# Decode step of a hybrid decoder: later loads and a split first block in the front stage, and an earlier third key load

## The reference

```
h = rms_norm(x) ; z = h @ w_in -> q_a(512), ckv(256), krope(64), u(512), qm(512), gate(2048)
q = rms_norm(q_a) @ w_q_b ; rope on q and krope ; ckv = rms_norm(ckv)
o_lat = softmax(q_lat.ckv + q_rope.krope) @ ckv     (8 heads; sample rows over a paged cache of 2048 keys)
pool  = (trailing means of u over 2, 4, 8, 16 rows - u) @ w_pool * pool_scale
mem   = rms_norm(mem_prompt) @ w_mem_kv -> k, v ; cross attention of qm (4 heads, 256 tokens)
x     = x + concat(o_lat @ w_v_b, pool, cross) * silu(gate) @ w_out ; y = rms_norm(x)
```

## Time and profile before

| what | value |
|---|---|
| median of three runs | 941.89 us |
| the profiled execution | 942.5 us, of which the span of the profile is 940.5 us and 2.0 us lie around it |
| TensorE matmuls | 917.1 us busy, 98% of the span |
| DVE, ACT, POOL | 531.7, 432.4, 43.8 us busy |
| DMA | 155.94 MB, mean 166 GB/s; some 400 GB/s in the first 38 us |

### The profile page before, as it was taken

The page is one execution under the profiler, slowest core; times in us unless marked ns, Lnnn a source line. Parts: engine busy times, 40 slices in busy tenths (PEclk is TensorE's granted clock), DMA queues, the critical chain, the costliest instruction groups (busy, mean ns, idle before and its releaser), DMA issues. The chain is left out here.

```text
span 940.5 us, 15369 instructions
## 1 busy us (share of the span) xinstructions
PE 917.1 (98%) x5649; PEld 826.2 (88%) x5649; DVE 531.7 (57%) x944; ACT 432.4 (46%) x735; POOL 43.8 (5%) x42
## 2 busy tenths in 40 slices
PE   6999999999999999999999999999999999999995
PEld 6999999999989899999999998888877888888884
DVE  6457444532475687887887558766576513134344
ACT  6764331122214566766677425677664413133301
POOL 0020003322000000000000000000100000000000
PEclk9999999999999999999999999999999999999998
DMA  9964452133452777777878626241350663224023
GB/s 363 327 241 157 134 192 92 68 111 115 174 214 98 225 241 227 237 235 229 253 236 250 224 98 220 79 146 34 117 214 28 213 213 100 80 89 157 1 90 112
DMA packets 75385, 155.94 MB, mean 166 GB/s; under 512 B 9176, under 2 KB 43545, under 8 KB 73320
## 3 DMA queue, kind: packets, MB, share of 16 engines
q1 hardware_dynamic: 74080, 147.98, 47.1%
q10 hardware_dynamic: 1232, 6.99, 2.0%
HBM read 143.56 MB, written 11.50 MB: 165 GB/s over the span
## 5 line engine op out<-in xcount | busy, mean ns | idle before, releaser
L67 PE MATMUL z<-x_hi,w_hi 128*128 128x288 f32 x512 | 153.6, 300 | 0.0
L68 PE MATMUL z<-x_lo,w_hi 128*128 128x288 f32 x512 | 150.8, 294 | 0.0
L69 PE MATMUL z<-x_hi,w_lo 128*128 128x288 f32 x512 | 150.8, 294 | 0.0
L184 ACT ACTIVATE w_hi<-w_raw 128x1024 fp32r<-128x1024 f32 (+2 forms) x62 | 64.9, 1046 | 157.8 <-PE z L69 69.3
L191 DVE TENSOR_TENSOR w_lo<-w_raw,w_hi 128x1024 fp32r<-128x1024 f32 (+2 forms) x62 | 76.8, 1239 | 76.4 <-ACT w_hi L184 76.0
L67 PEld LDWEIGHTS z<-x_hi,w_hi 128*128 128x128 f32 x512 | 96.0, 188 | 3.5 <-issue 1.1
L68 PEld LDWEIGHTS z<-x_lo,w_hi 128*128 128x128 f32 x512 | 96.1, 188 | 1.3 <-issue 0.2
L69 PEld LDWEIGHTS z<-x_hi,w_lo 128*128 128x128 f32 x512 | 96.0, 188 | 0.0
L1885 DVE TENSOR_TENSOR o_lo<-o_raw,o_hi 128x1024 fp32r<-128x1024 f32 x28 | 33.9, 1224 | 72.9 <-ACT o_hi L1735 72.8
L69 PE MATMUL z_acc<-x_hi,w_lo 128*128 128x288 f32 x256 | 75.1, 293 | 0.0
L1735 ACT ACTIVATE o_hi<-o_raw 128x1024 fp32r<-128x1024 f32 x28 | 29.5, 1059 | 72.5 <-PE pa_s L2367 26.7
(11 more groups left out here) (508 smaller groups left out, 2350.6 us busy)
## 6 DMA issues: line engine op xcount, KB each, us to landing
w_raw<-in_w_feat SPq DMA_DIRECT2D x56, 512.0 KB, 4.2
k_raw<-in_cache SPq DMA_DIRECT2D x128, 192.0 KB, 2.9
v_raw<-in_cache SPq DMA_DIRECT2D x128, 128.0 KB, 2.5
o_raw<-in_w_out SPq DMA_DIRECT2D x32, 512.0 KB, 4.1
w_raw<-in_w_mem_kv SPq DMA_DIRECT2D x16, 512.0 KB, 3.5
gate_spill<-gate_tmp SPq DMA_DIRECT2D x16, 288.0 KB, 3.2
mix<-gate_spill SPq DMA_DIRECT2D x4, 1152.0 KB, 10.4
x_nat<-in_x ACTq DMA_DIRECT2D x4, 1024.0 KB, 8.7
```

The source lines that it names most:

```text
L67: pe.matmul(out, a[0], b[0], start=start, stop=False)
L68: pe.matmul(out, a[0], b[1], start=False, stop=False)
L69: return pe.matmul(out, a[1], b[0], start=False, stop=stop)
L184: act.activation(hi_slot(s, u)[:, lo:w], s.wraw[:, u % RAW, lo:w], ACT.Copy).then_inc(s.w_hi, 1)
```

## The change

Five edits. (1) The first block of x is converted in two pieces, columns 0 to 255 and 256 to 575, on ACT and DVE, and TensorE waits for each apart. (2) Twelve products of ones (128 columns, float32, result never read) stand ahead of the first real product. (3) The natural rows are loaded from block 12 on, not from block 6, and their squares come later: row 0 at block 15, rows 1 and 2 in round 0, 3 and 4 in round 1, 5 and 6 in round 2. The mean moves to the end of round 1, root, reciprocal root, diagonal and `kv_z` to round 2, between its two memory blocks, and so does TensorE's spreading product. (4) The small tables, the pooling weights and the state are issued behind unit 8 on the sync queue, not ahead of unit 6. (5) In the middle stage quad 2 of the keys is loaded behind eight parts of `refill`, not twelve.

```diff
+FIRST_X, WARM = 2 * P, 12
 @@ sync, front
-                load_units(sp, a, s, 5, 6)
+                load_units(sp, a, s, 5, feat_unit(0) + 1)
                 for dst, src in ((psc[:], a["pool_scale_c"]),
...
-                for i in range(MIXED):
+                for i in range(1, MIXED):
 @@ scalar, front
-                        act.activation(xhi[:, k, :], xraw[:, k, :], ACT.Identity, scale=gx[:, k:k + 1]).then_inc(x_hi, 1)
-                        if k in (6, 7):
-                            load_row(k - 6)
+                        if k == 0:
+                            act.activation(xhi[:, 0, 0:FIRST_X], xraw[:, 0, 0:FIRST_X], ACT.Identity, scale=gx[:, 0:1]).then_inc(x0_hi, 1)
+                            act.activation(xhi[:, 0, FIRST_X:T], xraw[:, 0, FIRST_X:T], ACT.Identity, scale=gx[:, 0:1]).then_inc(x_hi, 1)
+                        else:
+                            act.activation(xhi[:, k, :], xraw[:, k, :], ACT.Identity, scale=gx[:, k:k + 1]).then_inc(x_hi, 1)
+                        if k in (12, 13):
+                            load_row(k - 12)
...
-                        if k in (11, 13, 15):
-                            square_row((k - 11) // 2)
+                        if k == 15:
+                            square_row(0)
...
-                    if i == 1:
+                    if i == 2:
                         act.wait_ge(chain, 1)
                         act.activation(rx[:, 2, :], rx[:, 1, :], ACT.Sqrt).then_inc(root, 1)
...
-                    if i == 0:
-                        square_row(3)
                     if i < 3:
-                        square_row(4 + i)
+                        square_row(2 * i + 1)
+                        square_row(2 * i + 2)
 @@ vector, front
                     memory(2 * i)
+                    if i == 2:
+                        dve.wait_ge(root, 2)
+                        rsqrt(dve, link, rx[:, 1, :], rx[:, 2, :], rx[:, 7, :], rx[:, 3, :])
...
                     memory(2 * i + 1)
...
-                    if i == 0:
+                    if i == 1:
                         dve.wait_ge(sq, TT)
                         link(dve.tensor_scalar(rx[:, 1, :], rx[:, 0, :], 1.0 / D, EPS, ALU.mult, ALU.add))
-                    if i == 1:
-                        dve.wait_ge(root, 2)
-                        rsqrt(dve, link, rx[:, 1, :], rx[:, 2, :], rx[:, 7, :], rx[:, 3, :])
 @@ tensor, front
+                pe.wait_ge(ident, 2)
+                for _ in range(WARM):
+                    pe.matmul(z[:, 0, 0, 0:P], s.ones[:], s.ones[:], start=True, stop=True)
                 for u in range(KV_UNITS):
                     latents(u)
                 for i in range(MIXED):
+                    memory(2 * i)
                     if i == 2:
                         pe.wait_ge(diag, TT)
...
-                    memory(2 * i)
 @@ sync, middle
-                refill(0, QPARTS)
+                refill(0, 8)
                 sp.wait_ge(normed, 8)
                 sp.wait_ge(roped, 4)
                 load_keys(2)
+                refill(8, QPARTS)
```

More of the change, by code:

```diff
@@ L255, in front_stage @@
         tail, tail_sb, st_in = sem("p_tail"), sem("p_tail_sb"), sem("p_state_in")
+        x0_hi, x0_lo = sem("p_x0hi"), sem("p_x0lo")
         w0_in, w0_hi, w0_lo, xs_hi, xs_lo, kv_low = sem("p_w0in"), sem("p_w0hi"), sem("p_w0lo"), sem("p_xshi"), sem("p_xslo"), sem("p_kvlow")
@@ L512, in _ @@
                         split_lo(dve, s, k // KV_K, k // KV_K + 1)
-                    dve.wait_ge(x_hi, k + 1)
-                    dve.scalar_tensor_tensor(out=xlo[:, k, :], in0=xraw[:, k, :], scalar=gx[:, k:k + 1],
-                                             in1=f32(xhi[:, k, :]), op0=ALU.mult, op1=ALU.subtract).then_inc(x_lo, 1)
+                    parts = ((slice(0, FIRST_X), x0_hi, x0_lo), (slice(FIRST_X, T), x_hi, x_lo)) if k == 0 else ((slice(0, T), x_hi, x_lo),)
+                    for cols, hi_done, lo_done in parts:
+                        dve.wait_ge(hi_done, k + 1)
+                        dve.scalar_tensor_tensor(out=xlo[:, k, cols], in0=xraw[:, k, cols], scalar=gx[:, k:k + 1],
+                                                 in1=f32(xhi[:, k, cols]), op0=ALU.mult, op1=ALU.subtract).then_inc(lo_done, 1)
                     if k % KV_K == KV_K - 1 or k == KD - 1:
@@ L541, in _ @@
                     memory(2 * i)
+                    if i == 2:
+                        dve.wait_ge(root, 2)
+                        rsqrt(dve, link, rx[:, 1, :], rx[:, 2, :], rx[:, 7, :], rx[:, 3, :])
+                        dve.wait_ge(ident, 3)
+                        for r in range(TT):
+                            dve.tensor_scalar(wide[:, P * r:P * r + P], s.ident[:], rx[:, 3, r:r + 1], None, ALU.mult).then_inc(diag, 1)
+                        dve.wait_ge(kv_raw, TT)
+                        for r in range(TT):
+                            m = rows(r)
+                            dve.tensor_scalar(s.kvn[0:m, r, :], s.kvn[0:m, r, :], rx[0:m, 3, r:r + 1], None, ALU.mult).then_inc(kv_z, 1)
                     memory(2 * i + 1)
@@ L640, in latents @@
                             wait_split(pe, s, u)
-                        pe.wait_ge(x_lo, k + 1)
+                        if k:
+                            pe.wait_ge(x_lo, k + 1)
+                        else:
+                            pe.wait_ge(x0_lo, 1)
                         for i in range(4):
+                            if k == 0 and P * i == FIRST_X:
+                                pe.wait_ge(x_lo, 1)
                             product(pe, kv_bank(i), (xhi[:, k, P * i:P * i + P], xlo[:, k, P * i:P * i + P]), w[kk], k == 0, k == KD - 1)
```

## The result

The changed kernel takes 947.33 us (median of six runs, 946.73 to 948.27), the kernel before, on the same chip, 941.97 us (six runs): ratio 1.0056, 95% interval 1.0047 to 1.0066. It is slower by 5.4 us, where 941.5 us was forecast: the sign and the place are those of the rival "unit 11 lands late", and the loss is larger. The profiled execution took 946.73 us (span 944.8), the lowest of its runs; that of before, 942.5 us (940.5), is above its median, so the two traces differ less, by 4.4 us (944.83 against 940.47 us).

What follows compares the result with a forecast made beforehand. TensorE, busy 98% of the span, was taken as the bound. half(2) 0.1 us later and 0.5 us gained at the keys made -0.4 us: 941.89 - 0.4 = 941.5 us; range for 8 in 10: 939.9 to 943.2 us.

Steps and rivals of the forecast that it cites:

- unit 11 lands late: Front-stage rival: tables and memory chunk issued just ahead delay unit 11's landing; over 943.8 us, 944.8 at T = 56; 7%.
- Edits 1 and 2: At the start: first real product at 6.6 us, 0.6 us earlier, clock raised early, TensorE 2.1 us ahead from block 2.
- The chain: Behind the squares, through ACT, DVE and GpSimd: half(2) can start at T + 19.9 us.
- T: Start of unit 11's high half on ACT: between 52.0 and 54.4 us, taken as 52.7.
- the two rivals on GpSimd: First rope operation: not held up by DVE, 940.2 us, 12%; or 3.37 us its own first-operation cost, 943.0 us, 8%.
- Edits 3 and 4 as a cover: In the saturated first stretch: fewer loads cover TensorE's running 2.1 us ahead, a gain of nothing by itself.
- Edit 5: Middle stage, third keys: TensorE's wait for k_lo at quad 2 goes, gaining 0.4 to 0.7 us, taken as 0.5.
- a wait of 2 us or so: New TensorE wait at half(2), for the low half of unit 14, given no price for the clock.

Runs made afterwards that it cites:

- tables_early: Changed kernel with small tables, pooling weights and state issued ahead of unit 6 again, as in the kernel before: 946.05 us, ratio 1.0037.
- state_first: Changed kernel with GpSimd's memset and four copies of the pooling state ahead of its rope operations: 943.16 us, ratio 1.0011.
- keys_only: Kernel before with only quad 2 of the keys loaded behind eight parts of refill: 941.26 us, ratio 0.9993.
- start_only: Kernel before with only the split first block and the twelve products of ones: 941.39 us, ratio 0.9995.
- mid_state_first: Changed kernel with the 64 sample rows on partitions 32 to 95, squared in two instructions, and state copies ahead of the rope: 943.00 us, ratio 1.0006.
- chain_only: Kernel before with only the natural rows, their chain and the small tables, pooling weights and state moved later: 949.41 us, ratio 1.0073.
- spread_tile: Changed kernel with the 64 sample rows loaded as 128 partitions of 1024 numbers, their sum of squares not the reference's: 945.00 us, ratio 1.0032.
- sample_first: Changed kernel with the 64-row natural tile loaded first, at block 12: 946.38 us, ratio 1.0048.
- rows_between: Changed kernel with the chain's old places, 64-row tile first, state copies ahead of rope, squares 1 and 2 between round 0's memory blocks: 942.01 us, ratio 1.0004.

## Why the prediction was wrong

- *Edits 1 and 2*: right in each number (6.61 us, the raised clock, 2.06 us ahead at unit 11's issue, `half(0)` over at 51.88 us). In the traces with the ones the clock rose at 4.2 to 7.4 us, in after at 4.7. That it varies from run to run is what the page of the Trainium skill quoted in the prediction, "TensorE: Matmul & The Clock Gate" (Part 1, What's actually happening), says. These traces agree, as far as one each of several kernels with the same start can; it cost no more than 0.4 us here (half the 0.74 us from the first product to the rise at 7.38 us in tables_early).
- *The chain*: right. T + 19.9 was forecast; 19.88, 19.90 and 19.87 us were measured with T at 56.95, 58.80 and 56.27. GpSimd's first rope operation took 1.83 us with one pair of DVE work beside it, where it took 3.37 with two: it is held up by DVE, and the two rivals on GpSimd fall. state_first showed that the chain runs through the copies.
- *T, the step that failed*: I let T lie at 54.4 us if the landing was unchanged, and chose 52.7 because a quarter of the bytes beside it was missing. That priced the tile by its bytes. On partitions 0 to 63 it slowed the packets beside it, and unit 11 took 11.3 us to land, not 8.8. With the shape taken away T was 54.66, so even then the upper end was right and the choice wrong by 2 us. The 8.8 us was a weak base too: with the same front, unit 11 took 5.6 us in the trace of keys_only. The rival priced T = 56 at 944.8 us and blamed the tables (in tables_early T hardly moved), and I gave it 7%.
- *The clock, missing from the sum*: I forecast a wait of 2 us or so and gave it no price beyond its length. It was 3.2 us long, and the lower clock behind it cost 1.4 us more, in two traces 2.7.
- *Edits 3 and 4 as a cover, "and a gain of nothing by itself"*: this holds only with them in place. Without them, in start_only, the start's gain is lost for two thirds, in `memory(0)`.
- *Edit 5*: right in kind, with one wait gone, that of the earlier trace rows, and too small: 0.5 us taken, 0.8 to 0.9 measured.

The sum again with measured terms, between the profiled executions: 4.4 (T and chain) + 1.4 (clock) - 0.8 (keys) - 0.6 (the wait at 491 us that only the trace of before has) = 4.4 us, the 4.4 us of the spans. The medians differ by 5.4; between the executions themselves it is 4.2. Of the 1.1 us between, 0.5 is that the trace of before was above its median and 0.6 that the trace of after was below its own.

What stays open: why weights land earlier or later from run to run, by 3 us for unit 11 between before and keys_only, whose fronts are the same. It may be the spread of 3.8 to 5.5 us in the runs with the ones and rows between the memory blocks, but only one trace of each was seen. Why the packets beside the tile weren't slow at once in before (159 ns) isn't known either.

## What to carry to other kernels

When a load is moved, ask what it does to the transfers beside it, by its shape and not by its bytes; look in the packet records for the same tile in its old place. When a change makes TensorE wait for some microseconds, read the granted clock behind such a wait and add its price, 1.4 us or more here. And a chain that begins at a landing should be cut where it runs through an engine that need not be in it: moving five GpSimd instructions gave back 4.2 us here.

## What was not expected of the hardware

- With a load to partitions 0 to 63 in flight (after) all 16 DMA engines together moved 217 to 221 GB/s; its packets took 563 ns, where the median in full tiles is 309, and the weight packets of another queue 280 ns, against 173 with the same 64 rows on partitions 32 to 95 (mid_state_first), where the rate was 399 GB/s.
- At the wait of 3.2 or 3.3 us ahead of `half(2)` the granted clock went to the lower level, for 3.4 us in three traces (after, chain_only, spread_tile) and 6.8 us in two (tables_early, sample_first); in rows_between, with a wait of 2.8 us, it stayed up.
